# The order of two matrix products in the last chunk of a tile, in a two-network fp32 kernel

## What is computed

```python
# shortened
def _conv_ffn(xn, w_up, conv_w, conv_b, w_down):      # first network, two times
    a, gval = jnp.split(xn @ w_up, 2, axis=-1)        # 1024 -> 2 * 2816
    a = conv3(a, conv_w) + conv_b                     # depthwise over the tokens
    return (jax.nn.gelu(a) * gval) @ w_down           # 2816 -> 1024

def conv_ffn(hn, w_in, conv_w, conv_b, w_out):        # second network, two times
    a, u = jnp.split(hn @ w_in, 2, axis=-1)
    a = causal_conv3(a, conv_w) + conv_b
    return (jax.nn.silu(a) * u) @ w_out
```

## Time and profile before

| | |
|---|---|
| median of 3 runs | 1501.7 us |
| span of the profiled execution | 1500.4 us |
| TensorE busy with matmuls | 1482.2 us, 10662 matmuls |
| VectorE, ScalarE, GpSimd busy | 1106.1, 776.8, 488.6 us |
| wide products (L595, 512 columns) | 2112 |
| half products (L595, 256 columns) | 2112 |
| products of `gemm` (L566) | 4788 |
| granted TensorE clock | nine tenths or more in every fortieth of the span |

### The profile page before, as it was taken

How to read it: one execution, slowest core, us unless ns; L and a number is a source line. 1 busy time by engine, 2 the same in 40 slices (tenths; PEclk the granted TensorE clock), 3 DMA queues, 4 the chain that set the end, 5 groups by cost and what they waited for, 6 DMA issues and landing times.

```text
span 1500.4 us, 24840 instructions
## 1 busy us (share of the span) xinstructions
PE 1482.2 (99%) x10662; PEld 1354.8 (90%) x10662; DVE 1106.1 (74%) x1156; ACT 776.8 (52%) x888; POOL 488.6 (33%) x295
## 2 busy tenths in 40 slices
PE   9999999999999999999999999999999998999997
PEld 7999999888888999999888889988888898988886
DVE  7747666788777557666888567978987568788853
ACT  6433544765544334444755456356664445665632
POOL 2306200245698408001254734002444000135410
PEclk9999999999999999999999999999999999999999
DMA  7674344555566563366555444334555534355552
GB/s 277 227 212 182 137 173 172 193 178 188 183 213 235 178 244 141 141 245 239 183 182 197 155 166 158 142 113 169 197 180 175 198 126 143 141 174 192 189 183 77
DMA packets 48589, 270.01 MB, mean 180 GB/s; under 512 B 11488, under 2 KB 14816, under 8 KB 19552
## 3 DMA queue, kind: packets, MB, share of 16 engines
q1 hardware_dynamic: 48480, 268.43, 50.8%
HBM read 261.59 MB, written 6.82 MB: 179 GB/s over the span
## 4 chain that ended last, share of the span: by engine, by line
PE 95%; DVE 3%; ACT 1%; DMA 1%; issue 0%; SPq 0%; DVEq 0%; ACTq 0%
PE gemm L566 38%; PE gemm L595 33%; PE aux L595 16%; DVE w_lo L1440 1%; PE aux L617 1%; PE aux L566 1%; PE gemm L676 1%; DMA h<-in_x 1%; PE aux L793 0%; PE gemm L678 0%; PE aux L653 0%; PE aux L666 0%; PE gemm L993 0%; PE aux L658 0%; ACT w_hi L1055 0%; PE aux L802 0%
## 5 line engine op out<-in xcount | busy, mean ns | idle before, releaser
L1440 DVE TENSOR_TENSOR w_lo<-raw,w_hi 128x2048 fp32r<-128x2048 f32 (+3 forms) x246 | 574.0, 2336 | 182.9 <-ACT w_hi L1055 180.2
L1055 ACT ACTIVATE w_hi<-raw 128x2048 fp32r<-128x2048 f32 (+3 forms) x246 | 457.0, 1858 | 308.7 <-PE gemm L566 184.2
L566 PE MATMUL gemm<-x_two,w_hi 128*128 128x256 f32 x1952 | 355.1, 284 | 0.0
L566 PEld LDWEIGHTS gemm<-x_two,w_hi 128*128 128x128 f32 x1952 | 303.6, 191 | 0.6
L566 PE MATMUL gemm<-x_two,w_lo 128*128 128x256 f32 x976 | 276.1, 283 | 0.0
L595 PE MATMUL gemm<-x_two,w_hi 128*128 128x512 f32 x672 | 234.6, 399 | 0.0
L2145 POOL TENSOR_TENSOR tmp<-tmp 128x512 f32<-128x512 f32 x24 | 38.9, 1622 | 477.2 <-ACT tmp L1082 463.2
L566 PEld LDWEIGHTS gemm<-x_two,w_lo 128*128 128x128 f32 x976 | 186.3, 191 | 0.0
L595 PE MATMUL gemm<-y_two,w_hi 128*128 128x512 f32 x528 | 185.3, 396 | 0.0
L2267 POOL TENSOR_TENSOR cv<-cv,rstd 128x512 f32<-128x512 f32 x44 | 116.6, 2649 | 179.3 <-ACT cv L1135 179.3
L595 PE MATMUL gemm<-x_two,w_lo 128*128 128x256 f32 x672 | 174.9, 281 | 0.0
(11 more groups left out here) (382 smaller groups left out, 2745.7 us busy)
## 6 DMA issues: line engine op xcount, KB each, us to landing
raw<-in_weights SPq DMA_DIRECT2D x222, 1024.0 KB, 4.8
raw<-in_weights SPq DMA_DIRECT2D x16, 768.0 KB, 4.2
raw<-in_weights SPq DMA_DIRECT2D x8, 512.0 KB, 4.3
raw<-in_weights SPq DMA_DIRECT2D x4, 576.0 KB, 3.6
s_inputs<-s_made SPq DMA_DIRECT2D x1, 2048.0 KB, 8.7
s_outputs<-s_cw SPq DMA_DIRECT2D x1, 2048.0 KB, 11.8
s_v<-s_inputs SPq DMA_DIRECT2D x1, 2048.0 KB, 9.8
s_cw<-s_outputs SPq DMA_DIRECT2D x1, 2048.0 KB, 10.6
```

What stands on the lines that cost most here:

```text
L566: mm = pe.matmul(out, lhs, rhs, start=fresh and m == 0, stop=end and m == 2, skip_group_check=True)
L1055: me.give(act.activation(w_hi[i % SPL][:, 0:n], raw[i % RAW][:, 0:n], ACT.Copy), w_hi_ready)
L1440: me.give(v.tensor_tensor(w_lo[i % RAW][:, 0:n], raw[i % RAW][:, 0:n], w_hi[i % SPL][:, 0:n].bitcast(F32), ALU.subtract), w_lo_ready)
```

## The change

In `gemm_halves` every chunk issues the wide product first and the half product second, the last chunk of a tile too. The `start` flag stays with the first wide product of a tile. Both products of the last chunk now carry `stop`. `mm_done` is raised by the last half product instead of the last wide one. No wait, transfer, buffer or product is added or removed.

```diff
                             wc, xc = pairs[k]
                             if xc in todo:
                                 me.take(*todo.pop(xc))
-                            wide = (dst[:, off:off + BANK], wh[:, wc, c0:c0 + P], both[:, xc, :, :])
-                            half = (dst[:, off:off + S], wl[:, wc, c0:c0 + P], both[:, xc, 0, :])
                             fresh, end = b.start and k == 0, b.stop and k == len(pairs) - 1
-                            for m, (out, lhs, rhs) in enumerate((half, wide) if end else (wide, half)):
-                                mm = pe.matmul(out, lhs, rhs, start=fresh and m == 0, stop=end and m == 1,
-                                               skip_group_check=True)
+                            pe.matmul(dst[:, off:off + BANK], wh[:, wc, c0:c0 + P], both[:, xc, :, :], start=fresh,
+                                      stop=end, skip_group_check=True)
+                            mm = pe.matmul(dst[:, off:off + S], wl[:, wc, c0:c0 + P], both[:, xc, 0, :], start=False,
+                                           stop=end, skip_group_check=True)
                 me.give(mm, mm_done)
```

## The result

The changed kernel has a median of 1505.45 us over 13 runs (1502.73 to 1506.10), the kernel before, run beside it, 1501.97 us (1501.65 to 1503.35). The ratio is 1.0020, with a 95% interval of 1.0013 to 1.0028: slower by 3.5 us, where +3.3 us and 1505.0 us were forecast. The profiled execution has a span of 1503.7 us against 1500.4.

The account below looks back on a forecast made before the run. TensorE, busy 99% of the span, was taken as the bound, through distances between product starts. Up and down block terms summed to 3.44 us, taken as +3.3 on 1501.7: 1505.0 us, range 1500.9 to 1505.9.

Parts of the forecast that it names:

- The bound: Whole kernel: TensorE busy 99% of the span, VectorE off the chain; FFN time is products times distance between starts.
- The entry: Behind the norm: all four FFNs start at 353.3 ns a pair (uneven), not 346.7 (even), and stay so.
- rival 2: Some FFNs even (346.7 ns a pair), others not: one gives 1501.6 us, two 1498.2 us; chance 0.12.
- Up blocks: 21 blocks behind the norm, 336 pairs: 353.3 instead of 352.5 ns a pair, +0.28 us an FFN.
- Down blocks of the first, third and fourth FFN: First group +0.02 us; three later groups go from 15.31 to 15.55 us each, together +0.72 us an FFN.
- Down blocks of the second FFN: S5 parts lie between them; most are uneven (353.3 ns a pair) already, so at most +0.1 us.
- Flags, and the half product as the last of a block: 208 more products with `stop`, and half products ending blocks: both taken as 0; failed cover would cost 12.5 us.
- Sum: All FFN terms: 3.44 us, less some rounding, taken as +3.3 us, giving 1505.0 us; chance 0.60.
- Rival 1: All FFNs hold 346.7 ns a pair (even) throughout: -9.6 us, 1492.1 us; chance 0.12.
- Rival 3: Neighbours do not matter: pair distances come from the place in the FFN, time stays 1501.7 us; chance 0.16.
- The page's rule: Matmul starts: columns over 2.4 GHz plus about 2.5 ns, 325 ns a pair in any order; the change does nothing.

Follow-up runs that it names:

- three reversals: Changed kernel with half product issued before wide one at pairs 3, 10 and 17 behind each FFN's norm: 1505.27 us.
- a single one: Changed kernel with half product issued before wide one only at pair 5 behind each FFN's norm: 1503.73 us.
- reversals in down blocks alone: Changed kernel with half product first again in the last chunk of each tile of down blocks, not of up blocks: 1502.55 us.
- four reversals: Changed kernel with half product issued before wide one at pairs 3, 10, 17 and 23 behind each FFN's norm: 1493.79 us.
- five and six reversals: Changed kernel, half product first at pairs 3, 10, 17, 23, 29 behind each FFN's norm: 1505.45 us; with pair 35 too: 1493.70 us.

## Why the prediction was right

- **The bound.** Right: no idle time before the FFN products, before or after, and what the FFNs gained or lost is in the distance of starts. (VectorE, called off the chain, holds 3% of it, nothing in the stretch of the first FFN.)
- **The entry.** All four FFNs of the profiled execution came out of the norm uneven, as forecast. This step was surer in the text than it should have been. Of the 28 entries of kernels without a reversal in the first up block, six are even: the first two FFNs with three reversals and with a single one, the second with six and with reversals in down blocks alone. So that none was even in the profiled execution is in part luck. The 1502.73 us of one run of the changed kernel would roughly fit one even FFN (rival 2 priced it at 3.4 us), but that run has no profile, so this is not shown.
- **Up blocks.** Forecast 0.28 us an FFN. Measured over 304 of the 336 pairs of the first: 107.42 - 107.16 = 0.26 us; over all 336 the trace has 0.26 to 0.28 us in each of the four.
- **Down blocks of the first, third and fourth FFN.** Forecast +0.02 us for the first group and +0.24 for a later one; measured 0.02 and 0.23. An FFN's four groups come to 0.74 to 0.76 us, forecast 0.74.
- **Down blocks of the second FFN.** Forecast at most +0.1 us; measured -0.37. The forecast took it that blocks that are uneven stay so. Behind three S5 parts TensorE ran even. What sets the course there is not shown.
- **Flags, and the half product as the last of a block.** Both taken as 0. The run with two flags and the old order shows the first. The second is shown by 15.55 us for a down group and 353.4 ns a pair in the up blocks, which leave no room for a late first product at a block's end.
- **Sum.** 3.3 us forecast; 3.3 us in span (1503.7 - 1500.4), 3.5 us between the medians. That the span meets the forecast to a tenth is luck. The FFNs have 3.0 us of it, 0.4 less than the terms of the sum give (3.44), all of this in the second FFN. Of the rest 0.26 us arose before the first FFN product, where both kernels are the same (before, then after):

```profile
266.40 0.40 PE L595 MATMUL aux<-x_two,w_hi 128*128 128x512 f32 x1
```

```profile
266.66 0.40 PE L592 MATMUL aux<-x_two,w_hi 128*128 128x512 f32 x1
```

  This start lies between 265.88 and 267.34 us in the ten profiles, so one pair of spans is good to about 1 us. The mechanism is shown by the courses and by the medians, not by this agreement.
- **Rival 1**, even throughout at 1492.1 us: not what this change does, but with the order set for it 1493.79 us was reached, 8.5 us below the kernel before where the rival had 9.6. The size was nearly right: 1.8 us an FFN in the up blocks (priced at 1.95, and pairs ahead of the fourth reversal are still uneven), 0.42 in the down blocks of the first, third and fourth (priced at 0.45).
- **Rival 3** fell with the runs that move reversals from one place to another.
- **The page's rule**: the Trainium skill, "TensorE: Matmul & The Clock Gate", section "Wait — 56ns, not 53.3ns?", gives one distance per column count. These runs disagree: the same two products take 346.7 or 353.3 ns at the same granted clock, and which of them is set by an exchange of instructions up to hundreds of pairs earlier.

## What to carry to other kernels

Where TensorE has no idle time, look at the distance between starts, not at busy time, and compare stretches of the same code: two values for one shape can be a gain that lies open, as the 8.5 us here. The mean length of a shape in a window (391 or 399 ns here) finds such stretches quickly. The alternating long and short products of this kernel hold a slower or a faster course for hundreds of instructions; a few exchanges, placed by the pattern of starts, choose it. An exchange at every tile end kept the up blocks, with a tile end every 8 pairs, from the fast one; in three of four down groups of three FFNs, with their tile ends 38 and 6 pairs apart, it led back to it. Whether other shapes do the same was not tried.

## What was not expected of the hardware

- The memory is long. With four reversals the even course lasts, in the first, third and fourth FFN, from pair 24 to the end of the last down block, some 490 pairs and 170 us, over all block ends and waits; in the second it ends with the S5 parts. In this time nothing that VectorE, ScalarE or the DMA queues do disturbs it: three pairs take 1.04 us throughout. In the uneven course they take 1.06 us throughout, likewise.
- The way out of the norm is not the same in each profile. The first distance behind it was 425 ns ahead of each of the six even entries in the profiles, and 418 to 421 ns ahead of all but two of the 34 uneven ones. The kernels with three and with four reversals have the same code up to there and for 23 pairs more, and their first FFNs show 425 and 421 ns. How often a kernel enters even seems to differ between kernels as well: 12 of 13 runs of the changed kernel lie within 1504.9 to 1506.1 us, 7 of 10 with reversals in down blocks alone within 1502.1 to 1502.7, near their profiled one, which has one even entry. What sets this is open.
- A perturbation can be undone by another six pairs later (five and six reversals), to within the uncertainty of the runs.

What stays open is the mechanism below this: what part of TensorE has the cycle of three pairs, and why 6.6 ns a pair are lost in it. The runs show the rule, not what lies beneath it. Whether `gemm`, at 120 ns for each 256 columns, sits in a slow course of its own was not tried.
